# Input projection of tiles 2 to 15 in pairs by Strassen's scheme, weight sums streamed; feed-forward's second pass in two groups

## Chip, core and metric

One core of one Trainium2 chip. The metric is device microseconds (us) of one launch, the median of three runs. Everything is float32. In the trace each program matmul stands as two records.

## What is computed

One decoder layer over a prompt of 2048 tokens and 32 sample tokens (8 sequences of 4), model width 1024. The part that the change touches is the combined input projection and, in the feed-forward, only how the columns of its second pass are grouped:

```python
hn = rmsnorm(x, norm1_g[l])
proj = hn @ w_in[l]                      # (T, 1024) @ (1024, 3608)
q_a, k_a, v_a, gate_a, low_a, qkv_b, z_b, beta_b, dec_b = jnp.split(proj, IN_IDX, axis=-1)
...                                      # GLA heads and gated delta-rule heads, chunk by chunk
x = x + mix @ w_out[l]
hn2 = rmsnorm(x, norm2_g[l])
up, ffn_new = causal_dwconv(hn2 @ w_up[l], st_ffn[l], ffn_conv_w[l])
a_f, b_f = jnp.split(up, [D_FF], axis=-1)
x = x + (jax.nn.silu(a_f) * b_f) @ w_down[l]
```

## The kernel before

There are two stages, the mixers and the feed-forward, each with one hand-written instruction stream per engine. No scheduler is in it: the order in the code is the order on each engine, and semaphores join the engines.

**Mixers.** The prompt is cut into 16 tiles of 128 tokens (t = 0 to 15), and a last short tile holds the 32 sample tokens. `mixer(t)` computes both head groups of a tile, carries the two states to the next tile, and is a long chain that goes back and forth between TensorE (PE), VectorE (DVE), ScalarE (ACT) and GpSimd (POOL). The names that matter, in the order of one tile on PE: the projected row block `proj` is turned (L764, L783); the previous tile's gated output is turned (L919, which waits for DVE L1721); ACT copies the turned columns to `cx` (L1192); DVE runs the convolution's four taps (L1505, then L1507 three times), between them the decays (L1535 to L1591); ACT and DVE make the SiLU (L1262, L1614); PE turns q (L840) and the last decay (L846); ACT copies it to `ked` (L1279); PE makes the GLA output (L859, L861) and the delta rule's products (L892, L896); then a ladder of seven steps inverts a triangular matrix, in each step PE (L930) and DVE (L1740, L1767, L1771) in turn; then `uu`, the output (L1037, L1038), the norm on ACT and DVE, and the gate L1721.

Between these steps stand fillers, `fill(i, j)`, that run slots i to j-1 of 40. A slot is two program matmuls (four records), and holds work that the chain doesn't need yet. In `mixer(t)` even slots below 16 hold the output projection of tile t-1 (L730), and the 8 odd ones and slots 16 to 39 hold the input projection of tile t+1 (L696): 32 slots, 64 program matmuls of 128x451, eight weight column groups of 8 matmuls each. The whole of `w_in` (14.8 MB) stays in SBUF, in `arena`. Groups go to two PSUM banks in turn, and ACT empties each of them once, with the norm's scale, straight into `proj` (L1153).

Tile 0 is projected ahead of everything while the weights arrive. Mixers 0 to 14 each host the projection of the next tile, mixer 15 hosts that of the 32 sample tokens (L714). SyncE (SP) issues all DMAs from one queue: the output weights are loaded again for each tile in 16 chunks of 256 KB into four buffers `wo`.

**Feed-forward.** The up-projection and the down-projection already go by Strassen's scheme, in two passes over 22 column tiles of the weights. The first pass has two groups of 256 columns, the second three groups of 176; each group has the same matmuls over its own columns (L2135), and a column tile takes 28 program matmuls of it in each group. The down-projection (L2209, 128x512) is the same in both.

## Time and profile before

| | us |
|---|---|
| median of 3 runs | 3298.98 (3298.91 to 3301.03) |
| the profiled execution, time | 3301.26 |
| the profiled execution, span of the trace | 3299.5 |
| PE busy | 3198.2 (97%) |
| DVE busy | 2063.4 (63%) |
| ACT busy | 859.1 (26%) |
| POOL busy | 581.5 (18%) |
| mean granted TensorE clock | 0.982 |

The span is one execution from its first to its last instruction. Up to about 1640 us it is the mixers, then the feed-forward. Busy shares are over the whole span. What an edit inside a tile is worth is read from the timelines of one tile. Times of a tile below are those of tile 7's mixer, which PE begins at 717.89 us with L919 of the tile before.

### The profile page before, as it was taken

What the parts mean: (1) busy time and instruction counts of PE and PEld (TensorE: products, weight loads), DVE (VectorE), ACT (ScalarE), POOL (GpSimd) and SP (SyncE); (2) the same over time, 40 slices, a digit from 0 to 9 for tenths busy, and PEclk for the clock granted to TensorE, in tenths of its full rate; (3) what the DMA queues carried; (4) which work ended last, traced back from release to release, by engine and by line L of the source; (5) the groups of instructions that cost most, each with busy time, mean ns of one, the idle gap of its engine ahead of it and who ended that gap; (6) DMA issues with size and microseconds to landing.
All of it is one profiled execution on the core that took longest, in us unless ns stands there. A gap on an engine that the chain in (4) does not pass through costs nothing.

```text
span 3299.5 us, 59597 instructions
## 1 busy us (share of the span) xinstructions
PE 3198.2 (97%) x23585; PEld 2178.1 (66%) x23585; DVE 2063.4 (63%) x4876; ACT 859.1 (26%) x1897; POOL 581.5 (18%) x945
## 2 busy tenths in 40 slices
PE   7999999999999999996799999999999999999999
PEld 3555555556555555554477777777768877888775
DVE  1566665655566665655566566666686666666668
ACT  1223333233223332232322111111232222222223
POOL 1111111111111111112231121111063112111110
PEclk9999999999999999997799999999999999999999
DMA  6022222222222212215531111111133111111112
GB/s 239 9 84 84 84 65 84 84 63 67 65 79 84 84 65 84 79 53 154 156 98 39 49 53 39 39 51 39 39 114 126 39 50 40 52 39 39 40 38 77
DMA packets 225314, 236.56 MB, mean 72 GB/s; under 512 B 14268, under 2 KB 169444, under 8 KB 225043
## 3 DMA queue, kind: packets, MB, share of 16 engines
q1 hardware_dynamic: 225043, 232.81, 22.4%
q8 instruction: 187, 3.06, 0.4%
q14 instruction: 84, 0.69, 0.1%
HBM read 203.10 MB, written 29.67 MB: 71 GB/s over the span
## 4 chain that ended last, share of the span: by engine, by line
PE 48%; DVE 1%; POOL 1%; ACT 0%; issue 0%; DVEq 0%; POOLq 0%
PE mlp_bank L2135 32%; PE mlp_bank L2209 15%; PE mlp_bank L2223 2%; DVE mcv L2577 0%; POOL acc L2457 0%; PE mlp_bank L2215 0%; POOL acc L2462 0%; DVE acc L2638 0%; ACT mcv L2298 0%; PE mlp_bank L2234 0%; PE mlp_bank L2221 0%; DVE raw L2521 0%; ACT mth L2312 0%; DVE mcv L2581 0%; ACT raw L2353 0%
## 5 line engine op out<-in xcount | busy, mean ns | idle before, releaser
L696 PE MATMUL mixer_bank<-arena,hnt 128*128 128x451 f32 x2048 | 868.0, 555 | 15.5 <-DMA arena<-in_w_in_dram 8.4
L2135 PE MATMUL mlp_bank<-arena,ws 128*128 128x176 f32 (+1 forms) x3520 | 657.6, 340 | 10.6 <-ACT raw L2325 9.0
L2135 PEld LDWEIGHTS mlp_bank<-arena,ws 128*128 128x128 f32 x3520 | 588.8, 190 | 49.0 <-ACT raw L2325 10.2
L696 PEld LDWEIGHTS mixer_bank<-arena,hnt 128*128 128x128 f32 x2048 | 367.4, 191 | 307.6 <-issue 302.6
L2209 PE MATMUL mlp_bank<-arena 128*128 128x512 f32 x1120 | 493.7, 592 | 0.0
L2610 DVE TENSOR_TENSOR acc<-acc,mlp_bank 128x512 f32<-128x512 f32 x560 | 370.5, 686 | 57.0 <-PE mlp_bank L2209 54.5
L2209 PEld LDWEIGHTS mlp_bank<-arena 128*128 128x128 f32 x1120 | 211.2, 190 | 231.7 <-issue 205.3
L2577 DVE SCALAR_TENSOR_TENSOR mcv<-raw,cf,mcv 128x512 f32<-128x512 f32 (+2 forms) x440 | 287.3, 670 | 68.5 <-ACT mcv L2298 58.2
L646 POOL TENSOR_TENSOR ex<-dtt,level 128x512 f32<-128x512 f32 (+1 forms) x114 | 142.9, 1253 | 939.8 <-DVE dtt L1645 641.6
L2135 PE MATMUL mlp_bank<-arena 128*128 128x176 f32 (+1 forms) x1320 | 254.9, 343 | 5.2 <-PEq L2720 4.3
L730 PE MATMUL mixer_bank<-wo,th 128*128 128x512 f32 x512 | 249.0, 609 | 3.0 <-DMA wo<-in_w_out_dram 2.4
L2135 PEld LDWEIGHTS mlp_bank<-arena 128*128 128x128 f32 x1320 | 224.1, 192 | 41.2 <-issue 26.3
L2135 PE MATMUL mlp_bank<-arena,wu 128*128 128x176 f32 (+1 forms) x1320 | 250.3, 339 | 0.9 <-ACT raw L2327 0.9
L2135 PEld LDWEIGHTS mlp_bank<-arena,wu 128*128 128x128 f32 x1320 | 221.8, 190 | 33.2 <-issue 19.1
L1153 ACT ACTIVATE proj<-mixer_bank,x_rs 128x451 f32<-128x451 f32 x128 | 81.2, 635 | 557.7 <-PE mixer_bank L696 525.8
L2521 DVE TENSOR_TENSOR raw<-raw,mlp_bank 128x176 f32<-128x176 f32 (+1 forms) x110 | 40.9, 372 | 275.2 <-PE mlp_bank L2135 275.2
L2298 ACT ACTIVATE mcv<-raw,cf 128x512 f32<-128x512 f32 (+2 forms) x220 | 139.8, 637 | 100.7 <-DVE raw L2521 80.0
L2281 ACT COPY raw<-mlp_bank 128x176 f32<-128x176 f32 (+1 forms) x110 | 36.5, 332 | 493.2 <-PE mlp_bank L2135 493.2
L730 PEld LDWEIGHTS mixer_bank<-wo,th 128*128 128x128 f32 x512 | 93.3, 191 | 100.6 <-issue 89.2
L1507 DVE SCALAR_TENSOR_TENSOR cv<-cx,cw,cv 128x128 f32<-128x128 f32 x576 | 154.9, 348 | 0.0
L2515 DVE TENSOR_TENSOR raw<-raw,mlp_bank 128x176 f32<-128x176 f32 (+1 forms) x110 | 40.8, 371 | 151.2 <-ACT raw L2327 151.2
L1767 DVE TENSOR_TENSOR qe<-qe,mixer_bank 128x256 f32<-128x256 f32 x80 | 33.9, 423 | 126.9 <-PE mixer_bank L930 126.9
(368 smaller groups left out, 3619.3 us busy)
## 6 DMA issues: line engine op xcount, KB each, us to landing
wo<-in_w_out_dram SPq DMA_DIRECT2D x260, 256.0 KB, 2.7
arena<-in_w_up_dram SPq DMA_DIRECT2D x44, 512.0 KB, 4.9
wu<-in_w_up_dram SPq DMA_DIRECT2D x44, 512.0 KB, 4.9
arena<-in_w_down_dram SPq DMA_DIRECT2D x40, 512.0 KB, 4.1
arena<-in_w_in_dram SPq DMA_DIRECT2D x7, 1804.0 KB, 16.2
xc<-in_x_t_dram SPq DMA_DIRECT2D x16, 512.0 KB, 4.2
xt<-in_x_prompt_dram SPq DMA_DIRECT2D x16, 512.0 KB, 4.9
xr<-in_x_prompt_dram SPq DMA_DIRECT2D x16, 512.0 KB, 3.8
```

Source lines behind the costliest of these rows:

```text
L646: gp.tensor_tensor(ltm[0:N, :, 0:N], lt[0:N, :, 0:N], level[0:N, l, 0:N].unsqueeze(1).to_broadcast([N, H, N]), ALU.mult)\
L696: x = pe.matmul(bank[ring(g)][0:N, 0:GW], hnt[:, k, 0:N], w[:, k, g * GW:(g + 1) * GW], start=(k == 0), stop=(k == KT - 1))
L730: pe.matmul(bank[e if t == TILES else 0][0:N, :], mixt[k // H][:, k % H, 0:N], wo[i % 4][:, :], start=(k == 0), stop=(k == KT - 1)).then_i ...
L1153: act.activation(proj[0:N, g * GW:(g + 1) * GW], bank[ring(g)][0:N, 0:GW], ACT.Identity, scale=x_rs[0:N, :]).then_inc(s_proj_out, 1)
L1507: x = dve.scalar_tensor_tensor(out=dst, in0=src, scalar=cw[:, c, tap:tap + 1], in1=dst, op0=ALU.mult, op1=ALU.add)
L2135: x = pe.matmul(out[:, 0:N], left[:, k, :], xb[:, slot, k, g * N:(g + 1) * N], start=first and k == 0, stop=k == HK - 1, skip_group_check= ...
L2209: pe.matmul(bank[4 + o % 4][:, :], left, right, start=True, stop=True).then_inc(s_down_done, 1)
L2223: x = pe.matmul(out[0:N, :], act_[a + j][:, t * C:t * C + N], right[j][:, e * 512:e * 512 + 512], start=(j == 0 and t < 8), stop=(j == 1))
L2298: act.activation(cv[e][:, 0:n], raw[p][e][:, c0:c0 + n], ACT.Identity, scale=cf[p][:, e, 0:1])\
L2521: dve.tensor_tensor(v, v, q_bank[:, 0:N], ALU.add).then_inc(s_q2_added, 1)
L2577: x = dve.scalar_tensor_tensor(out=dst, in0=src, scalar=w, in1=dst, op0=ALU.mult, op1=ALU.add)
L2610: dve.tensor_tensor(v, v, bank[4 + o % 4][:, :], ALU.add).then_inc(s_y_added, 1)
```

## The change

**The projection.** Tiles 2 to 15 are projected in pairs (2,3), (4,5), ... as a 2 x 2 block product: rows are the two tiles, the inner dimension and the columns are halved. Seven products of 4 program matmuls of 128x451 take the place of eight, for each of four column group pairs. Mixer 2p hosts two of them and mixer 2p+1 the other two: 14 products, 56 program matmuls and 28 slots a mixer, for 64 and 32 before. Mixers 0 to 13 host (`HOSTS = 14`). Tiles 0 and 1 are projected the plain way ahead of mixer 0 (`project_first`, 128 program matmuls), mixers 14 and 15 host only the sample tokens.

**Weights.** Only the lower half of the columns stays in SBUF. The four combinations T1 to T4 of each column group are made once by DVE (16 subtractions of 128x1804) and stored to DRAM, and each mixer streams ten chunks of 924 KB (T1 to T4 and B22, for two groups) through a ring of four buffers.

**Activations.** POOL makes the seven left operands of a pair in eight instructions of 128x512 (`x_operands`), which now also takes the norm's scale, read back from DRAM. In the queue of POOL they stand between mixers 2p-1 and 2p. DVE scales the two tiles' columns by the norm's gain together, at the end of an even mixer.

**Results.** Of each 7 products ACT copies 4 blocks to a staging buffer (`keep`), and DVE adds 3 (`add_product`). Finished blocks are stored to DRAM and `proj` is loaded from there a tile later; of the odd mixers' results the first row's blocks are written to `proj` at once.

**Slots.** Slots 0, 1, 2, 3, 4, 6, 8 and 10 hold the output projection, 28 others the products; slots 13, 19, 23 and 39 are empty.

**Feed-forward.** The second pass goes in two groups of 264 columns.

The diff, cut to its core:

```diff
+HOSTS = TILES - 2
+PRODUCTS = 14
+CHUNKS = 10
+OUT_SLOTS = {0: 0, 1: 1, 2: 2, 3: 3, 4: 4, 6: 5, 8: 6, 10: 7}
+PRODUCT_SLOTS = {slot: p for p, slot in enumerate([5, 7, 9, 11, 12, 14, 15, 16, 17, 18, 20, 21, 22, 24] + list(range(25, 39)))}
...
+            def x_operands(p):
+
+                c, done = 2 * p + 2, 7 * p
+                a11, a12, a22, s1, s2, s3, s4 = (xops[:, b, :, :] for b in range(7))
+                scale = [rsb[:, e, :].unsqueeze(1).to_broadcast([C, HK_IN, C]) for e in range(2)]
+                gp.wait_ge(s_rsb_loaded, 16 * (p + 1))
+                gp.wait_ge(s_xg_made, p + 1)
+                if p:
+                    gp.wait_ge(s_products, PRODUCTS * 2 * p)
...
+                gp.tensor_tensor(a11, xc[:, 0:HK_IN, :], scale[0], ALU.mult).then_inc(s_xops_made, 1)
...
             for t in range(1, TILES):
                 mixer(t, t + 1, False, True)
+                if t % 2 and t < HOSTS - 1:
+                    x_operands((t + 1) // 2)
...
+                for k in range(2 * half, 2 * half + 2):
+                    x = pe.matmul(out[:, 0:GW], xops[:, left, k, :], right[:, k, :], start=first and k == 0,
+                                  stop=k == HK_IN - 1, skip_group_check=not first)
...
+            def keep(t, q, block, source):
+
+                act.wait_ge(s_products, PRODUCTS * t + q + 1)
...
+                act.copy(stage[4 * (q // 7) + block], bank[source][:, 0:GW]).then_inc(s_kept, 1)
...
-                fill(1)
+                if not sample:
+                    act.wait_ge(s_halo_kept, n + 1)
                 if out and not sample:
-                    act.wait_ge(s_halo_kept, n + 1)
                     y_square(t, C)
+                    act.wait_ge(s_y_normed, 3 * t - 2)
+                front(0)
...
                     if a == 1 and out and not sample:
-                        if not last_prompt:
-                            keep_y_half(t, C, 0)
+                        keep_y_half(t, C, 0)
...
+                    if half == 0:
+                        pe.wait_ge(s_sg_new, t + 1)
+                    else:
+                        pe.wait_ge(s_hs_half, t)
+                    y_turn(t, C, half)
...
                 conv_tap(2)
+                if hosts:
+                    make_c11(t, 0)
...
-        PASSES = ((0, 2, 256, 0, 8), (T // 2, 3, 176, 8, 9))
+        PASSES = ((0, 2, 256, 0, 8), (T // 2, 2, 264, 8, 9))
```

**Where it stands on the engines.** First PE, from the product with `qka` (L827 before, L1099 now) to the first GLA product (L859 before, L1135 now). L696 before and L970 now are the slots' matmuls, two to a slot; L840 and L1114 turn q, L846 and L1120 the last decay. Before:

```order
L827 MATMUL mixer_bank<-qka 32x32 x16
L696 MATMUL mixer_bank<-arena,hnt 128x451 x4
L840 MATMUL mixer_bank<-ident,cv 128x128 x4
L696 MATMUL mixer_bank<-arena,hnt 128x451 x4
L846 MATMUL mixer_bank<-ident,ex 128x128 x2
L850 MATMUL mixer_bank<-ident,cv 128x128 x4
L696 MATMUL mixer_bank<-arena,hnt 128x451 x2
L859 MATMUL mixer_bank<-va,at 128x128
```

and now:

```order
L1099 MATMUL mixer_bank<-qka 32x32 x16
L970 MATMUL mixer_bank<-arena 128x451 x4
L1114 MATMUL mixer_bank<-ident,cv 128x128 x4
L970 MATMUL mixer_bank<-arena 128x451 x2
L1120 MATMUL mixer_bank<-ident,ex 128x128 x2
L1126 MATMUL mixer_bank<-ident,cv 128x128 x4
L970 MATMUL mixer_bank<-arena 128x451 x2
L1135 MATMUL mixer_bank<-va,at 128x128
```

Slot 19 is gone between L1114 and L1120; slot 13 is gone a little earlier.

Second ACT, from the table load after the decay's exponential to the copy of `ked` (L1279 before, L1578 now), which the GLA product waits for. L1153 empties a projection bank, L1158 and L1448 square the layer's output, L1420 squares the input tokens of a later tile (before: L1139, in the ladder). Before:

```order
L1266 ACT_TABLE_LOAD
L1153 ACTIVATE proj<-mixer_bank,x_rs 128x451 [waits x_rsed,proj_done,va_copied]
L1158 ACTIVATE cx,y_ss<-yo 128x8x128 [waits out_out,halo_kept]
L1273 ACTIVATE th<-mixer_bank 128x512 [waits q_turned]
L1163 ACTIVATE y_ln<-y_ss,eps 128x1 [waits y_squared]
L1279 COPY ked<-mixer_bank 128x256 [waits sg_done,kl_turned]
```

and now:

```order
L1563 ACT_TABLE_LOAD
L1448 ACTIVATE cx,y_ss<-yo 128x8x128 [waits out_out,halo_kept]
L1420 ACTIVATE cx,x_ss<-xt 128x8x128 [waits x_loaded,y_normed]
L1572 ACTIVATE th<-mixer_bank 128x512 [waits q_turned]
L1453 ACTIVATE y_ln<-y_ss,eps 128x1 [waits y_normed]
L1578 COPY ked<-mixer_bank 128x256 [waits sg_done,kl_turned]
```

The emptying of a bank has left this place, and the square of the input tokens has come ahead of `ked`.

Third POOL, from the last ladder step of an odd mixer to the next mixer's first two instructions (L629 and L636 before, L825 and L832 now). Before there was nothing between them. Now:

```order
L842 TENSOR_TENSOR ex<-dtt,level 128x512 [waits p_done,lt_made] x2
L849 MEMSET qe 128x4x64 [waits dx_done]
L861 TENSOR_TENSOR arena<-xc,xt 128x512 [waits products,xg_made,rsb_loaded]
L862 TENSOR_TENSOR hnt<-hnt,xt 128x512
L863 TENSOR_TENSOR arena<-xc,xt 128x512
L864 TENSOR_TENSOR arena<-hnt,xt 128x512
L866 TENSOR_TENSOR arena<-hnt,arena 128x512 [waits xops_made]
L868 TENSOR_TENSOR arena<-arena 128x512 [waits xops_made]
L869 TENSOR_TENSOR arena<-arena,hnt 128x512
L871 TENSOR_TENSOR arena<-arena 128x512 [waits xops_made]
L825 COPY va<-proj 128x512 [waits sg_done,og_done,proj_loaded,blocks_added]
L832 TENSOR_TENSOR ug<-incl,gg 128x512 [waits grow_done,g_made,masks_made]
```

Eight instructions wait for the odd mixer's last product (`products`) and stand ahead of the even mixer's `ug`.

## Rows read from the trace of the kernel before

**Rows 1.** Windows: span, its length, busy us per engine, granted clock, DMA share, GB/s.

```profile
0.00:80.00 80.00, 62.16 (x172) 31.64 (x173) 11.52 (x38) 16.30 (x37) 12.71 (x46) 0.92 0.72 246
710.00:800.00 90.00, 89.31 (x954) 52.73 (x953) 57.63 (x174) 26.15 (x55) 12.94 (x15) 1.00 0.24 77
1520.00:1530.00 10.00, 5.89 (x232) 5.08 (x232) 5.29 (x16) 0.96 (x2) 3.13 (x5) 0.50 0.59 172
```

**Rows 2.** Timeline of PE, one tile: start, length, instruction, idle before and releaser.

```profile
717.89 0.66 PE L919 MATMUL mixer_bank<-ident,th 128*128 128x128 f32 x4 [0.39 <-DVE th L1721]
...
753.79 0.60 PE L840 MATMUL mixer_bank<-ident,cv 128*128 128x128 f32 x4
...
759.42 0.38 PE L859 MATMUL mixer_bank<-va,at 128*128 128x128 f32 x2
...
771.97 0.45 PE L930 MATMUL mixer_bank<-ex,qe 128*32 128x16 f32 x32
```

**Rows 3.** Timeline of DVE, the same tile.

```profile
718.88 0.57 DVE L1472 TENSOR_TENSOR drel<-proj,dtb 128x4 f32<-128x4 f32 x1
...
720.87 2.44 DVE L1505 TENSOR_SCALAR cv<-cx,cw 128x128 f32<-128x128 f32 x12 [1.21 <-ACT cx L1192]
...
724.13 0.90 DVE L1535 TENSOR_TENSOR qe<-qe 128x256 f32<-128x256 f32 x1
...
750.83 1.90 DVE L1614 SCALAR_TENSOR_TENSOR cv<-th,cv 128x512 f32<-128x512 f32 x3 [0.86 <-ACT th L1262]
...
767.95 1.20 DVE L1749 TENSOR_TENSOR qe<-ident,qe 128x512 f32<-128x512 f32 x1
...
771.51 0.41 DVE L1740 TENSOR_TENSOR ex<-mixer_bank,nbeta 128x256 f32<-128x256 f32 x1
```

**Rows 4.** Timeline of ACT, the same tile.

```profile
755.74 0.64 ACT L1153 ACTIVATE proj<-mixer_bank,x_rs 128x451 f32<-128x451 f32 x1
756.27 1.05 ACT L1158 ACTIVATE cx<-yo 128x1024 f32<-128x1024 f32 x1
...
757.98 0.37 ACT L1279 COPY ked<-mixer_bank 128x256 f32<-128x256 f32 x1
...
772.41 1.06 ACT L1139 ACTIVATE cx<-xt 128x1024 f32<-128x1024 f32 x1
```

**Rows 5.** Timeline of POOL, the same tile.

```profile
717.95 1.48 POOL L629 COPY va<-proj 128x512 f32<-128x512 f32 x1 [18.17 <-ACT proj L1153]
723.71 1.04 POOL L636 TENSOR_TENSOR ug<-incl,gg 128x512 f32<-128x512 f32 x1 [4.28 <-DVE gg L1525]
...
767.32 1.27 POOL L646 TENSOR_TENSOR ex<-dtt,level 128x512 f32<-128x512 f32 x1 [2.28 <-PE mixer_bank L946]
```

**Rows 6.** Timelines of PE and ACT, the last prompt tile.

```profile
1458.95 0.66 PE L919 MATMUL mixer_bank<-ident,th 128*128 128x128 f32 x4 [0.39 <-DVE th L1721]
...
1501.48 0.77 PE L859 MATMUL mixer_bank<-va,at 128*128 128x128 f32 x2 [4.04 <-ACT ked L1279]
...
1521.04 1.97 PE L755 MATMUL mixer_bank<-ident,xr 128*128 128x128 f32 x8 [4.72 <-ACT proj L1411]
...
1555.93 1.11 PE L919 MATMUL mixer_bank<-ident,th 128*128 128x128 f32 x4 [3.35 <-DVE th L1721]
...
1496.39 2.59 ACT L1411 ACTIVATE proj<-mixer_bank,x_rs 32x451 f32<-32x451 f32 x4
```

**Rows 7.** PE at the start, and line L787: duration, first and last start.

```profile
8.43 8.63 PE L696 MATMUL mixer_bank<-arena,hnt 128*128 128x451 f32 x16 [8.43 <-DMA arena<-in_w_in_dram]
...
34.21 36.60 PE L696 MATMUL mixer_bank<-arena,hnt 128*128 128x451 f32 x96
...
L787 PE MATMUL mixer_bank<-lowt,wa x68: 270/270/396, 73.3 to 1558.9; 16*128 16x128 f32 x64, 16*128 16x32 f32 x4
```

**Rows 8.** Chain of waits in the feed-forward: start, length, group.

```profile
1758.54 20.72 PE mlp_bank L2135 x96
...
2540.19 22.68 PE mlp_bank L2135 x152
```

More of the change, by code:

```diff
@@ L43 @@
 GROUPS = 8
+FIRST = [(g, tile) for g in (4, 0, 5, 1, 6, 7) for tile in range(2)] + [(2, 1), (3, 1), (2, 0), (3, 0)]
 PARTS = 4 * GROUPS
 GW = NIN // GROUPS
+HW = NIN // 2
+HK_IN = KT // 2
+HOSTS = TILES - 2
+PRODUCTS = 14
+CHUNKS = 10
+KEPT = 8
+ADDED = 6
+KEEP_OF = {0: 1, 2: 2, 3: 3, 6: 4, 7: 5, 9: 6, 10: 7, 13: 8}
+ADD_OF = {1: 1, 4: 2, 5: 3, 8: 4, 11: 5, 12: 6}
+FIRST_GROUPS = 2 * GROUPS
+P_T1, P_T2, P_T3, P_T4, P_B22 = range(5)
+A11, A12, A22, S1_X, S2_X, S3_X, S4_X = range(7)
+C11, C12, C21, C22 = range(4)
+OUT_SLOTS = {0: 0, 1: 1, 2: 2, 3: 3, 4: 4, 6: 5, 8: 6, 10: 7}
+PRODUCT_SLOTS = {slot: p for p, slot in enumerate([5, 7, 9, 11, 12, 14, 15, 16, 17, 18, 20, 21, 22, 24] + list(range(25, 39)))}
 O_QA, O_VA, O_GA, O_LOW, O_QKV, O_Z, O_BETA, O_DEC = 0, 512, 1024, 1536, 1552, 3088, 3600, 3604
@@ new lines, in store_block @@
+            def store_block(t, j, block):
+                b = 4 * j + block
+                if block == C11:
+                    sp.wait_ge(s_added, ADDED * t + ADD_OF[(1, 8)[j]])
+                elif block == C12:
+                    sp.wait_ge(s_added, ADDED * t + ADD_OF[(5, 11)[j]])
+                elif block == C22:
+                    sp.wait_ge(s_added, ADDED * t + ADD_OF[(4, 12)[j]])
+                else:
+                    sp.wait_ge(s_kept, KEPT * t + KEEP_OF[(6, 13)[j]])
+                c0 = HW * (block in (C12, C22)) + column_group(t, j) * GW
+                tile = t - t % 2 + 2 + (block in (C21, C22))
+                sp.dma_start(p_d[tile, :, c0:c0 + GW], stage[b]).then_inc(s_stage_stored, 16)
@@ L847, in mixer @@
                 x.then_inc(s_kl_turned, 1)
+                if not sample:
+                    pe.wait_ge(s_out_out, 2 * t)
                 for h in range(H):
@@ L1326, in mixer @@
                     norm_k()
-                    fill(3)
-                    front(0)
+                    if hosts:
+                        keep(t, 6, C21, 1)
+                    front(1)
                     inverse_rms(0, front)
-                for g in range(4, GROUPS - 1):
-                    fill(g)
+                if hosts:
+                    keep(t, 7, C11, 0)
+                    keep(t, 9, C22, 0)
+                    keep(t, 10, C12, 1)
+                if t == TILES - 1:
+                    keep_sample()
                 if sample:
```

815 lines of the change are left out of this document (540 added, 275 removed).

## The prediction

> **What bounds the kernel now.** I read the windows first. In a middle stretch of the mixers PE is busy 89.31 of 90 us at full clock, DVE 57.6, ACT 26, POOL 13 [rows 1]. That looks like a kernel bound by PE, in which each slot removed is won. The timelines of one tile say more. Its period is (1458.95 - 717.89) / 8 = 92.63 us [rows 2, 6]. A slot is four records of 36.6/96 = 0.38 us, 1.52 us [rows 7]. The question at each removed slot is how late the chain behind it would be if PE came 1.52 us earlier. So I looked, at each of the four places, for when DVE or ACT had finished what PE then used, and beside it at the last prompt tile, whose slots are almost empty, and which shows the chain bare [rows 6]. The reader should see that PE arrives only about 1 us after its data, and at two places after them.
>
> **The tile, place by place.** The change takes 4 of 32 slots from a tile, 6.06 us of PE.
>
> Slot 13 lies ahead of L840. DVE starts the taps at 720.87, after waiting for ACT, and then has work without a real break until L1614 ends at 750.83 + 1.90 = 752.73; PE comes at 753.79 [rows 2, 3]. The slack is 1.06. The change also puts the first C11 addition between the taps: a 128x451 operation is a little under the 0.7 of 128x512, 0.6. So the data are there at 753.3, and L840 moves by 0.5, not 1.5.
>
> Slot 19 lies ahead of L859, which needs `ked`. It is done at 757.98 + 0.37 = 758.35, and PE comes at 759.42 [rows 2, 4]. On ACT one emptying leaves this path (L1153, 0.53 by the starts), and the squares of the input tokens enter it (L1139's 1.06, and a short wait for the instruction ahead), which before ran at 772, where nobody waited [rows 4]. With the 0.6 from DVE: 758.35 + 0.6 - 0.5 + 1.1 = 759.5. L859 stays where it was, and both slots are lost. The last tile bears this out: there, with hardly any filler, PE waited 4.04 us for `ked`, 2.59 of it for ACT's sample blocks, and L859 came 1501.48 - 1458.95 = 42.5 us after L919, against 41.5 in the full tile [rows 2, 6].
>
> Slot 23 lies in the ladder's second step. L1740 ends on DVE at 771.92, and PE goes on at 771.97 [rows 2, 3]: DVE is the bound there already, and the slot gives nothing. Behind it `turn_y(1)` now waits for DVE's `hs_half`, which follows L1740, the new C12 addition (0.6) and a 128x512 operation: PE goes on at about 773.1 where it did at 772.65, +0.4. From there to the end of the ladder the same 13 slots stand in both kernels.
>
> Slot 39 lies ahead of L919, which waits for DVE as it is (0.39) [rows 2]. The wait becomes 1.9.
>
> So a hosted tile takes 92.63 + 0.1 + 0.4 = about 93.0 us (0.1 is from `ked`): nothing is won inside a tile. The other additions on DVE and copies on ACT lie in gaps of the ladder; C22 ahead of product 13 is one product behind its data, and the turn of `uu` (0.9 us) stands between. They cost nothing while DVE is idle there.
>
> **POOL's eight instructions.** In six of the tiles (2, 4, ... 12) they start when the odd mixer's last product ends, about 2.5 us ahead of L919, and run 8 x 1.27 = 10.2 us [rows 5]. In this time DVE runs the gate, the decay's start and the taps, on the chain. What the rows show of the two engines: L1472, four elements wide, starts at 718.88 and ends at 719.45, when POOL's copy ends (717.95 + 1.48 = 719.43); L1749 ends 0.56 after POOL's L646 at 768.59; L1535 ends at 725.03, 0.28 after POOL's L636 at 724.75 [rows 3, 5]. Each waited to the end of the POOL instruction. The bounds are 1 us a tile (POOL slips between) and 7 us (all eight block DVE, 10.2 less the 3 us in which DVE waits for ACT before the taps, now that the 1.2 us scaling has left the odd mixer's end). I take 5: about five of the eight fall on a working DVE at 1 us each. 6 x 5 = +30 us. `ug` comes later as well, at about 729 for 727.6; PE has 1.7 us to spare up to L840 and DVE is later still, so it adds nothing.
>
> The Trainium skill, "SBUF — State Buffer", section "Who interferes with whom", says that DVE's second port pair is shared with GpSimd and held exclusively for a whole instruction, by DVE operations with two SBUF inputs and also by `tensor_scalar` in a two-port mode. All three rows have two SBUF inputs; no row here shows the second kind. By it the twelve `tensor_scalar` taps of L1505 would be blocked too, and a tile would cost about 6 in place of 5; without it, about 3.5.
>
> **The ends of the mixers.** Now tile 0 alone is projected first, and L787 of tile 0 comes at 73.3 [rows 7]. After the change 256 records stand ahead of it: 8.4 start, 256 x 0.38 = 97.1, 2.5 for the low clock of the first 16 records (8.63 for 6.1), some 3 for the second tile's columns and the second group, 2.7 for the turns: 114, so +41. The loads (14.8 MB at 246 GB/s, 60 us [rows 1]) are covered. DVE's 16 subtractions, 1.9 us each by the same rate, wait for projections and stores and end by about 111, just in time; bounds of this part +36 to +46.
>
> Against it stand the last mixers. Before: 15 tiles from 73.3 to the last L787 of a prompt tile at 1460.97, and 97.9 to 1558.9 [rows 7]. Now mixers 14 and 15 have no filler. Their length is read from tile 15: 1555.93 - 1458.95 = 97.0, less the 4.7 us wait for sample blocks (L755 now goes to another bank) and the 2.6 of L1411 ahead of `ked`: 90 each [rows 6]. It is at a granted clock down to 0.50 in its second half [rows 1], to which PE fell after its idle stretches; if the clock stayed up, 80. Sum: 114 + 91.7 (mixer 0, which has no output projection and takes that now) + 13 x 93.0 + 2 x 90 = 1594.7, against 1558.9: +36.
>
> **Feed-forward.** A record takes 20.72/96 = 215.8 ns at 256 columns and 22.68/152 = 149.2 to 149.8 at 176 [rows 8]. At 264 it is 215.8 + 8 x 0.83 = 222.5. A column tile has 168 records of 176, 25.1 to 25.2 us, and then 112 of 264, 24.9: 0.2 x 22 = 5 us less (bounds +3 to -8 for the turn between the passes and the longer last group). -5.
>
> **Sum.** 36 + 30 - 5 = +61 on the profiled execution's 3301.3, that is 3362; the median is 2.3 below that execution, so 3360.
>
> **The rivals.**
> 1. *PE is the bound after all.* The busy share of 89.31 in 90 speaks for it, the waits at L840, L859, L930 and L919 against it. If every slot is won, a tile takes 86.6 and mixer 0 85.6, and POOL is hidden: 114 + 85.6 + 13 x 86.6 + 180 = 1505, -54, and -5: 3240. This is the faster side; it decides from 2.6 us a tile, at which the start-up's +36 is paid. 0.09.
> 2. *POOL slips into DVE's gaps.* Three tenths of the first 10 us are DVE waiting. 6 x 1 in place of 6 x 5: 3336. 0.25.
> 3. *The stream disturbs the chain.* DMA carries 77 GB/s, 7.1 MB a tile [rows 1]; the change adds ten chunks of 0.92 MB and 2.8 MB of blocks, to 19 MB or 206 GB/s. Rows show 246 at a share of 0.72, so it fits on average. But the 16 output weight chunks of 256 KB, with four buffers, are now used in a row in slots 0 to 4, behind a 924 KB chunk in the one queue (3.8 us at 246). If that makes PE more than the 1.7 us late that L840 forgives, say by 3 more a tile: 13 x 3 = +39, 3399. 0.14.
> 4. *Half of it.* The chain is tight at L840 and L919, but the token squares fit, and two slots are won: 13 x 3 = -39 and POOL at 3: about 3305, on either side of no change. 0.08.
>
> The forecast has 0.44. The range 3300 to 3400 holds it, rivals 2 and 3 and half of 4. A measurement tells 0.2% (6.6 us) from no change: slower has 0.44 + 0.25 + 0.14 = 0.83, same 0.04 and faster 0.13 (rival 1 and half of 4).
>
> **What would show it.** L787 of tile 0 at about 114. In a hosted tile PE waits: about 1 us at L1114 for DVE, 2 at L1135 for ACT's `ked`, 1 in the ladder's second step, 2 at L1196 for the gate; PE at 93% rather than 99%. An even tile longer than an odd one by about 5 us, with DVE operations that end when POOL's do. If odd and even tiles are alike, POOL's term is wrong; if an odd tile is under 90 us, the chain's is. Waits on `wo` at L1002 show rival 3.

## The result, and the profile after

The changed kernel takes 3429.4 us (median; 3424.3 to 3434.0), against 3298.9 for the kernel before on the same chip: a ratio of 1.0393, 95% interval 1.0380 to 1.0405. It is slower, as forecast, but the loss is 130 us where 61 were expected, and 3429 lies above the range of 3300 to 3400. The profiled execution's span is 3425.8.

The page of the changed kernel, its first parts. Columns: busy us and share of each engine; then the granted clock in 40 slices.

```profile
span 3425.8 us, 56382 instructions
...
PE 3186.7 (93%) x22129; PEld 2094.5 (61%) x22129; DVE 2132.8 (62%) x4778; ACT 825.7 (24%) x1743; POOL 640.9 (19%) x985
...
PEclk9899999999999999988689999999999999999999
```

PE is busy for 93% of the span, as the forecast said. The clock's digit is 9 through the hosted mixers, and 9 stands for 90% or more: too coarse for a few per cent. Windows are finer. These are the changed kernel's: the hosted mixers 1 to 13, mixer 0, one odd and one even tile. (Where only PE was asked for, the columns are start and end, length, PE busy, granted clock, DMA share, GB/s; else all engines stand between, as in [rows 1].)

```profile
222.90:1505.60 1282.70, 1185.29 (x12339) 0.96 0.58 188
...
111.00:222.90 111.90, 79.47 (x911) 48.16 (x910) 66.66 (x181) 23.66 (x51) 19.04 (x19) 0.83 0.64 212
809.60:908.40 98.80, 90.65 (x950) 54.24 (x949) 61.04 (x179) 26.14 (x55) 15.73 (x18) 0.96 0.55 177
908.40:1010.70 102.30, 92.61 (x951) 54.85 (x950) 66.02 (x181) 26.91 (x57) 18.77 (x21) 0.94 0.62 201
```

And the same stretch of hosted mixers in the kernel before:

```profile
164.60:1369.00 1204.40, 1195.45 (x12548) 1.00 0.24 75
```

Before, PE ran through the mixers at a granted clock of 1.00. After, it gets 0.96 on average. In 13 tiles PE has 209 records fewer, its busy time falls by only 10 us, and the stretch is 78 us longer. The sum of the forecast held PE at full clock throughout the hosted tiles.

The waits of PE in the hosted mixers 1 to 13 of the changed kernel (instruction, what it waited for: us in total, times, longest):

```profile
PE mixer_bank L1135 <- ACT ked L1578: 26.4, 13, 2.1
PE mixer_bank L1196 <- DVE th L2068: 24.7, 13, 1.9
PE mixer_bank L1065 <- DVE gg L1866: 12.5, 6, 3.8
PE mixer_bank L1027 <- DVE hgla L2042: 10.5, 13, 0.8
PE mixer_bank L1207 <- DVE ex L2087: 10.1, 13, 0.8
```

The same list of the kernel before has 5.1 us ahead of L919 (13 times 0.4) and 2.1 ahead of L930, and nothing else. All waits of the changed kernel's list add up to 96 us. Four of the five shown were forecast: about 2.1 us for `ked` in twelve of the 13 tiles (1.1 in the last) and 1.9 for the gate in each, under 1 at the two ladder steps. The fifth, for `gg`, stands in even tiles alone and is told below. The first record of each mixer (L1059, L787 before) gives the tile lengths, of one execution of each kernel:

| stretch, us | before | forecast | after | fillers (e3) | bound (e12) |
|---|---|---|---|---|---|
| start, to the first L1059 | 73.3 | 114 | 111.0 | 111.0 | 111.3 |
| mixer 0 | 90.8 | 91.7 | 111.9 | 112.1 | 103.6 |
| odd hosted tiles, mean of 7 | 92.6 | 93.0 | 97.0 | 93.7 | 94.1 |
| even hosted tiles, mean of 6 | 92.6 | 98.0 | 100.6 | 99.0 | 93.8 |
| mixers 1 to 13 together | 1204.2 | 1239 | 1282.7 | 1250.2 | 1221.5 |
| mixer 14 | 92.6 | 90 | 95.9 | 97.8 | 80.5 |
| mixer 15 | 97.3 | 90 | 90.4 | 86.5 | 89.8 |
| from there to the end | 1741.2 | 1736.2 | 1733.9 | 1737.4 | 1737.8 |
| span | 3299.5 | 3360.9 | 3425.8 | 3395.0 | 3344.6 |

(e3 and e12 are told below.) Of the 65 us by which the span missed the forecast, 43.7 lie in the hosted mixers, 20.2 in mixer 0, 6 in mixers 14 and 15; the start and the feed-forward give 5 back.

**What a clock loss looks like in rows.** PE's timeline in mixer 7 of the changed kernel, from the wait for `ked`; it answers to the row of L859 in [rows 2]:

```profile
849.94 0.46 PE L1135 MATMUL mixer_bank<-va,at 128*128 128x128 f32 x2 [2.12 <-ACT ked L1578]
...
851.35 0.63 PE L1135 MATMUL mixer_bank<-va,at 128*128 128x128 f32 x2
...
853.06 1.88 PE L1168 MATMUL mixer_bank<-cv 128*128 128x128 f32 x8
854.76 1.06 PE L1172 MATMUL mixer_bank<-cv 128*128 128x128 f32 x8
...
866.24 4.27 PE L970 MATMUL mixer_bank<-arena 128*128 128x451 f32 x8
...
893.94 3.25 PE L970 MATMUL mixer_bank<-arena 128*128 128x451 f32 x8
```

PE waits 2.12 us and runs on for 1.4 us. Then eight records of the delta rule's products take 1.88 us (L1168), and the next eight, of the same shape, 1.06 (L1172). Eight records of the projection take 4.27 us at 866 and 3.25 at 894. No wait stands inside these rows: the records themselves are longer. Windows show why (start and end, length, PE busy, granted clock, DMA share, GB/s):

```profile
851.40:854.70 3.30, 3.30 (x18) 0.50 0.00 0
854.80:858.20 3.40, 3.40 (x23) 1.00 0.00 0
```

For these microseconds the granted clock is the lower of its two levels, 1.2 in place of 2.4 GHz. This cost stands in no list of waits. It has to be read from the clock column, or from one shape that has two durations.

Read in this way, the clock of mixers 1 to 13 of the changed kernel falls 26 times, for 3 to 7 us each time: ten times at the wait for the gate, five behind the wait for `ked`, eight in the ladder's first steps, three at the wait for `gg` where that is 2.5 us or more. Together it is at the lower level for 115 of the 1282.7 us.

**Even tiles.** DVE's timeline of the even mixer 8, and POOL's beside it; they answer to [rows 3] and [rows 5]:

```profile
907.00 1.20 DVE L1816 TENSOR_SCALAR dabs<-drel 128x4 int32<-128x4 int32 x1
909.39 6.86 DVE L1846 TENSOR_SCALAR cv<-cx,cw 128x128 f32<-128x128 f32 x12 [1.19 <-ACT cx L1482]
```

```profile
904.13 1.58 POOL L861 TENSOR_TENSOR arena<-xc,xt 128x512 f32<-128x512 f32 x1 [16.00 <-PE mixer_bank L970]
...
913.51 1.32 POOL L871 TENSOR_TENSOR arena<-arena 128x512 f32<-128x512 f32 x1
```

The twelve `tensor_scalar` taps take 6.86 us where [rows 3] have 2.44, while the second half of POOL's eight instructions runs, to 914.83. So it is in each even tile that has them, 6.0 to 6.9, and in no other (2.44). PE then waits 3.8 us for `gg` (L1065), and 0.8 to 3.8 in the six tiles. The Trainium skill, "SBUF — State Buffer", section "Who interferes with whom", names `tensor_scalar` in a two-port mode as one that GpSimd can block. No row of the kernel before showed that; this one agrees, with 4.4 us on twelve instructions.

**Mixer 0.** SP's, DVE's and ACT's timelines of the changed kernel, 60 to 140 us (SPq is the queue in which SP issues DMAs). DVE waited for the stores of the weight sums, and the last sum ended at 118.71 + 4.11 = 122.8, where the forecast had 111:

```profile
63.77 19.10 SPq L509 DMA_DIRECT2D sums_d<-arena  x6
...
94.24 28.92 SPq L509 DMA_DIRECT2D sums_d<-arena  x10
123.20 0.46 SPq L622 DMA_DIRECT2D proj_d<-ex  x1
```

```profile
78.41 4.11 DVE L1730 TENSOR_TENSOR arena<-arena 128x1804 f32<-128x1804 f32 x2 [26.57 <-DMA sums_d<-arena]
...
118.71 4.11 DVE L1730 TENSOR_TENSOR arena<-arena 128x1804 f32<-128x1804 f32 x2 [3.60 <-DMA sums_d<-arena]
134.05 0.16 DVE L1860 SCALAR_TENSOR_TENSOR drel<-drel,dln 128x4 f32<-128x4 f32 x1 [8.58 <-ACT dln L1499]
```

```profile
132.76 0.63 ACT L1490 ACTIVATE qe<-mixer_bank,ba 128x128 f32<-128x128 f32 x2 [20.89 <-DMA proj_d<-qe]
```

Then DVE waited 8.58 us for ACT, ACT for the store of tile 1's projection out of `ex` and `qe`, and this store stood in SP's queue behind the last ten stores of the sums. PE waited 22.7 us at L1065.

### The profile page after: what moved, and what is told of

It is laid out like the page before. It is cut to its first block and busy times, and to the rows that moved or that the text cites. A ratio compares the mean times of both kernels' runs of the same rounds, so it can differ in the third digit from the quotient of the medians.

```text
span 3425.8 us, 56382 instructions
## 1 busy us (share of the span) xinstructions
PE 3186.7 (93%) x22129; PEld 2094.5 (61%) x22129; DVE 2132.8 (62%) x4778; ACT 825.7 (24%) x1743; POOL 640.9 (19%) x985
## 5 line engine op out<-in xcount | busy, mean ns | idle before, releaser
L970 PE MATMUL mixer_bank<-arena 128*128 128x451 f32 x1568 | 677.3, 562 | 0.4 <-issue 0.4
L2496 PE MATMUL mlp_bank<-arena,ws 128*128 128x256 f32 (+1 forms) x2816 | 648.3, 383 | 9.6 <-ACT raw L2686 9.6
L2496 PEld LDWEIGHTS mlp_bank<-arena,ws 128*128 128x128 f32 x2816 | 536.0, 190 | 92.8 <-ACT raw L2686 10.4
L970 PEld LDWEIGHTS mixer_bank<-arena 128*128 128x128 f32 x1568 | 281.6, 194 | 210.4 <-issue 204.3
L2938 DVE SCALAR_TENSOR_TENSOR mcv<-raw,cf,mcv 128x512 f32<-128x512 f32 (+2 forms) x352 | 264.5, 767 | 59.4 <-ACT mcv L2659 50.6
L1002 PE MATMUL mixer_bank<-wo,th 128*128 128x512 f32 x512 | 266.3, 651 | 18.0 <-DMA wo<-in_w_out_dram 17.1
L2496 PE MATMUL mlp_bank<-arena 128*128 128x256 f32 (+1 forms) x1056 | 249.1, 386 | 5.3 <-PEq L3084 4.4
L2496 PE MATMUL mlp_bank<-arena,wu 128*128 128x256 f32 (+1 forms) x1056 | 246.0, 383 | 0.9 <-ACT raw L2688 0.9
L2496 PEld LDWEIGHTS mlp_bank<-arena 128*128 128x128 f32 x1056 | 201.1, 191 | 57.0 <-issue 26.4
L2882 DVE TENSOR_TENSOR raw<-raw,mlp_bank 128x256 f32<-128x256 f32 (+1 forms) x88 | 37.5, 426 | 276.7 <-PE mlp_bank L2496 276.7
L1444 ACT COPY arena<-mixer_bank 128x451 f32<-128x451 f32 x112 | 59.7, 533 | 592.4 <-PE mixer_bank L970 592.3
L1002 PEld LDWEIGHTS mixer_bank<-wo,th 128*128 128x128 f32 x512 | 100.6, 208 | 142.8 <-issue 96.5
L2876 DVE TENSOR_TENSOR raw<-raw,mlp_bank 128x256 f32<-128x256 f32 (+1 forms) x88 | 37.5, 426 | 191.3 <-ACT raw L2688 191.3
L2642 ACT COPY raw<-mlp_bank 128x256 f32<-128x256 f32 (+1 forms) x88 | 33.1, 377 | 493.2 <-PE mlp_bank L2496 493.2
```

Of the source, the lines that this page charges most:

```text
L970: x = pe.matmul(out[:, 0:GW], xops[:, left, k, :], right[:, k, :], start=first and k == 0, stop=k == HK_IN - 1, skip_group_check=not first)
L1002: pe.matmul(bank[e if t == TILES else 3 + e][0:N, :], mixt[k // H][:, k % H, 0:N], wo[i % 4][:, :], start=(k == 0), stop=(k == KT - 1)).th ...
L1444: act.copy(stage[4 * (q // 7) + block], bank[source][:, 0:GW]).then_inc(s_kept, 1)
L2496: x = pe.matmul(out[:, 0:N], left[:, k, :], xb[:, slot, k, g * N:(g + 1) * N], start=first and k == 0, stop=k == HK - 1, skip_group_check= ...
L2876: dve.tensor_tensor(v, v, q_bank[:, 0:N], ALU.add).then_inc(s_q1_added, 1)
L2938: x = dve.scalar_tensor_tensor(out=dst, in0=src, scalar=w, in1=dst, op0=ALU.mult, op1=ALU.add)
```

## The experiments

Twelve kernels ran, each beside runs of the kernel before. The changed kernel's 3429.4 is the reference for those made from it.

### e1: POOL's eight operations made small

```diff
-                a11, a12, a22, s1, s2, s3, s4 = (xops[:, b, :, :] for b in range(7))
+                a11, a12, a22, s1, s2, s3, s4 = (xops[:, b, 0:1, 0:4] for b in range(7))
...
-                gp.tensor_tensor(a11, xc[:, 0:HK_IN, :], scale[0], ALU.mult).then_inc(s_xops_made, 1)
+                gp.tensor_tensor(a11, xc[:, 0:1, 0:4], scale[0], ALU.mult).then_inc(s_xops_made, 1)
...
```

> POOL's eight instructions of x_operands are made four columns wide in place of 128x512; the left operands of the products are otherwise left unmade, so the projections of tiles 2 to 15 are not the reference's. All waits and their order stay. Theory A (an even tile is longer because DVE's taps wait for these instructions, and PE then for DVE): L1846 back from 6.9 to 2.4 us in even tiles, the wait for gg at L1065 gone, even tiles as long as odd ones; 6 x 3.5 = 21 us at least, with the lower clock behind the wait some 30: 3395 to 3410 for 3429. Rival (the even tiles are longer through their DMAs, the 1.8 MB reload of proj among them): no change, 3425 to 3433.

3417.0 us (ratio 1.0346, 1.0329 to 1.0363): 12 us less, not 21 or more, so it lies between the two expectations. DVE's taps came back to 0.28 us each (0.29 at the most), 2.44 for the twelve in every tile, and the wait for `gg` is gone, so the mechanism is right. Even tiles became 2.9 us shorter and odd ones did not: they take 97.7 and 97.8 now (odd ones 97.0 in the changed kernel), at a granted clock of 0.96, the changed kernel's. The price at a full clock is measured by e11.

### e2: the token squares back at their old place

```diff
                 if out and not sample:
                     y_square(t, C)
-                    act.wait_ge(s_y_normed, 3 * t - 2)
-                front(0)
...
                     if hosts:
                         keep(t, 6, C21, 1)
+                    front(0)
                     front(1)
```

> The square of the input tokens goes back on ACT from ahead of ked to where it stood before, behind the last copy ahead of the ladder. Theory A: ked is 1.1 us earlier, the wait at L1135 falls from 2.1 to 1.0 us, 14 tiles: -15 us, and a shorter wait lowers the clock less: 3400 to 3415. Rival (the wait at L1135 is late by something other than ACT's row of work, the turn of q for instance): the wait stays at 2.1 and the time at 3429.

3410.0 us (1.0332, 1.0315 to 1.0349), 19 less, as theory A has it. The wait for `ked` fell from 26.4 to 11.9 us in 13 tiles, 1.1 us a tile, just the length of the moved square (1.06). The hosted mixers are 19.5 us shorter; the other 5 come with a clock of 0.97 for 0.96 and aren't taken apart further.

### e3: useless matmuls in PE's waits

```diff
+            def warm(count, b=0):
+                for _ in range(count):
+                    pe.matmul(bank[b][:, GW:512], ident[:, :], lo[:, 0, 0:512 - GW], start=True, stop=True,
+                              skip_group_check=True)
...
+                if 2 <= t < HOSTS and t % 2 == 0:
+                    warm(16)
...
```

> Nothing is taken away: useless matmuls of 128x61 from the identity into unused bank columns are added on PE in hosted tiles where it waits now: 8 ahead of L1135, 3 in the second ladder step, 7 ahead of L1196, 16 ahead of L1065 in even tiles. Theory A (the excess over the forecast is the granted clock, which falls behind each wait): granted clock in hosted tiles from 0.95 to 0.98 or more, hosted tiles 2 to 4 us shorter, 3380 to 3405, though PE does more. Rival (the clock costs nothing, since the tile is bound by the chain; the excess is DMA): the added 0.2 us pieces are hidden or lengthen the chain, 3429 to 3440.

3402.5 us (1.0318, 1.0301 to 1.0335), as theory A has it. The kernel has 348 program matmuls (696 records) more than the changed one, none of use, and is 27 us faster. The matmuls write into banks that hold open products, so only its time is read. Its hosted mixers (start and end, length, PE busy, granted clock, DMA share, GB/s):

```profile
223.10:1473.30 1250.20, 1207.09 (x13000) 1.00 0.60 193
...
802.40:896.10 93.70, 91.22 (x986) 1.00 0.57 188
896.10:995.30 99.20, 94.57 (x1018) 1.00 0.64 206
```

The clock is 1.00 again, and now an odd tile takes 93.7 and an even one 99.0, against 93.0 and 98.0 forecast. The clock was thus worth 32.5 of the 43.7 us by which the hosted mixers missed, by one execution of each kernel; between the medians of the two kernels lie 27 us. The traffic is as high as in the changed kernel (193 against 188 GB/s), so it is not what brings the clock down. The fillers don't set the tile's length themselves: right behind them PE still waits, 0.4 us for `ked` and 0.4 for the gate.

### e4: the stream made small

```diff
...
-                sp.dma_start(x_flat[n % 4], t_d[4 * what + j]).then_inc(s_ring_loaded[n % 4], 16)
+                sp.dma_start(x_flat[n % 4][:, 0:64], t_d[j, :, 0:64]).then_inc(s_ring_loaded[n % 4], 16)
```

> The ring's chunks of 924 KB are loaded as 64 columns of it (33 KB) each, in the same places of SP's queue and with the same semaphores; most of the right operands stay stale, so the projections of tiles 2 to 15 are not the reference's. Theory A: the stream explains little: the waits on wo at L1002 go, 0.5 to 1 us a tile at most, 3410 to 3429. Rival B (rival 3 of the prediction: the stream makes the output weights late and pushes the chain): 3 us a tile and more, 3375 to 3390.

3429.8 us (1.0400, 1.0382 to 1.0417), no change, with 101 GB/s in the hosted mixers for 188. Rival 3, the stream that disturbs the chain, falls. Its sign was missing in the changed kernel too: L1002 waited on `wo` once in these 13 mixers, for 0.6 us.

```profile
220.90:1503.10 1282.20, 1190.97 (x12338) 0.95 0.33 101
```

### e5: slots 13 and 19 filled, 22 and 24 empty

```diff
-PRODUCT_SLOTS = {slot: p for p, slot in enumerate([5, 7, 9, 11, 12, 14, 15, 16, 17, 18, 20, 21, 22, 24] + list(range(25, 39)))}
+PRODUCT_SLOTS = {slot: p for p, slot in enumerate([5, 7, 9, 11, 12, 13, 14, 15, 16, 17, 18, 19, 20, 21] + list(range(25, 39)))}
```

> The changed kernel with the products of slots 14 to 24 put on 13 to 21: slots 13 and 19 are filled, 22 and 24 stand empty. Theory A (slot 19 lies ahead of the wait for ked, 2.12 us in every tile, and slots 22 and 24 where no wait ends late): the wait for ked falls from 2.12 to about 0.4, as with the fillers, a hosted tile gets 1.5 us shorter and some more by the clock, 3395 to 3412 against 3429.4. Rival B (the work taken from 22 and 24 opens waits of the same length in the ladder of a=1 to 3, one wait goes and two come): no change or worse, 3425 to 3436.

3415.3 us (1.0350, 1.0332 to 1.0367), 14 less, inside neither span of the two expectations. Both theories were half right. These are its waits in the hosted mixers:

```profile
PE mixer_bank L1207 <- DVE qe L2096: 12.2, 13, 0.9
...
PE mixer_bank L1257 <- DVE qe L2087: 6.7, 13, 0.5
```

The wait for `ked` is gone from the list; two in the ladder came, 0.8 and 0.5 us more a tile. All waits add up to 81 us, 15 less than in the changed kernel. The clock did not rise: 0.95.

### e7: tile 1's store ahead of the last sums

```diff
             store_sum(11, P_T2, 3, y_flat[3])
+            sp.wait_ge(s_one_out, GROUPS)
+            sp.dma_start(p_d[1, :, 0:5 * GW], ex_[:, 0:5 * GW]).then_inc(s_stage_stored, 16)
+            sp.dma_start(p_d[1, :, 5 * GW:NIN], qe_[:, 0:3 * GW]).then_inc(s_stage_stored, 16)
             store_sum(12, P_T3, 2, x_flat[2])
...
```

> The changed kernel with the store of tile 1's first projection ahead of the stores of sums 12 to 15 in SyncE's queue. Theory A (in mixer 0 VectorE waited 8.6 us for ScalarE, which waited for that store, and TensorE 22.7 us for VectorE): the 8.6 us go, mixer 0 takes 103 for 111.9, the time is 3419 to 3424. Rival B (VectorE then waits for the stores of the sums instead, which come later): mixer 0 stays at 110 or more, 3427 to 3433.

3423.9 us (1.0371, 1.0354 to 1.0389), at the end of theory A's range; its four runs spread from 3419 to 3432, so the median alone does not carry the verdict. The trace does: mixer 0 takes 103.7 for 111.9, and PE's wait for `gg` there is 14.2 for 22.7, 8.5 less. In this execution the hosted mixers take 4 us more than the changed kernel's and mixer 14 3, which hides it in the time.

### e9: w_out's pieces ahead of the re-loaded w_in

```diff
-            for g in range(4, GROUPS):
-                w_group(g)
             wo_chunks(t - 1, 20)
+            for g in range(4, GROUPS):
+                w_group(g)
             load_proj(t + 1)
```

> The changed kernel with w_out's pieces of mixer 14 ahead of the four re-loaded groups of w_in in SyncE's queue, nothing else. Theory A (SyncE needs 12 us to issue the 3.6 MB of w_in, and they fill the DMA engines, while TensorE waits 14.0 us for a piece of w_out): that wait goes, mixer 14 takes 81 for 95.9, the time is 3413 to 3418. Rival B (the groups then come too late for the sample's second half in mixer 15, or the load of proj does): mixer 15 grows by what mixer 14 gives back, 3425 to 3432.

3417.6 us (1.0362, 1.0341 to 1.0383), 12 less, as theory A has it. In the changed kernel PE stood 14 us in mixer 14:

```profile
1526.45 5.74 PE L1002 MATMUL mixer_bank<-wo,th 128*128 128x512 f32 x8 [14.01 <-DMA wo<-in_w_out_dram]
```

With the edit this wait is gone and mixer 14 takes 81.5 for 95.9; mixer 15 takes 93.4 for 90.4, so 11 are left.

### e8: holes in the kernel before

All work kept; one product is done a slot later, one a slot earlier.

```diff
+                    late = {19: (), 20: (19, 20), 37: (37, 38), 38: ()}
-                    for part in range(i, j):
+                    for part in [p for slot in range(i, j) for p in late.get(slot, (slot,))]:
```

> The kernel before, all its work kept, with two holes in TensorE's stream of the kind that the change makes: the product of slot 19 is done with that of slot 20, and that of slot 38 with that of slot 37, so that TensorE has nothing to do at the places where it stands ahead of gla_out (L859) and ahead of turn_mixed(1) (L919). Each hole is about one slot, 1.5 us, so 3.0 us a tile and 43 us in 14 tiles are waited whatever the clock does. Theory A (in the changed kernel the granted clock falls because TensorE stands still for one or two us at a time): the clock of the hosted tiles, 1.00 in the kernel before, falls to 0.97 to 0.99, a tile takes 97 to 98 for 92.6, and the time is 3355 to 3380. Rival B (the clock fell in the changed kernel for something else that came with it, its traffic or its other matmuls): the clock stays at 1.00, a tile takes 95.6, and the time is 3340 to 3344.

3339.1 us (1.0122, 1.0106 to 1.0137). By the time alone rival B would nearly have won, 3340 to 3344. The trace says otherwise. Only one of the two holes opened: the wait ahead of L919 became 1.9 us (0.4 before), and no wait for `ked` appears, so 1.5 us a tile are waited and not 3.0. The expectation had read the order wrongly: slot 20 lies ahead of L859 too, so the product moved there from slot 19 left no hole.

```profile
PE mixer_bank L919 <- DVE th L1722: 24.8, 13, 1.9
```

Yet nine tiles of thirteen are 2.6 to 3.9 us longer (95.2 to 96.5), one 2.3, and only three 1.5 (94.1 or 94.2). One tile of each kind, by windows (start and end, length, PE busy, granted clock, DMA share, GB/s):

```profile
260.40:356.10 95.70, 93.50 (x967) 0.98 0.24 73
353.20:356.50 3.30, 3.30 (x16) 0.50 0.32 85
737.40:831.50 94.10, 91.89 (x966) 1.00 0.24 74
735.80:739.10 3.30, 3.30 (x21) 1.00 0.30 80
```

The short windows are the microseconds behind the wait. And PE's timeline behind two of these waits:

```profile
352.76 0.81 PE L919 MATMUL mixer_bank<-ident,th 128*128 128x128 f32 x4 [1.90 <-DVE th L1722]
353.36 2.77 PE L783 MATMUL mixer_bank<-ident,proj 128*128 128x128 f32 x12
356.06 0.92 PE L787 MATMUL mixer_bank<-lowt,wa 16*128 16x128 f32 x4
...
735.36 0.66 PE L919 MATMUL mixer_bank<-ident,th 128*128 128x128 f32 x4 [1.90 <-DVE th L1722]
735.85 1.60 PE L783 MATMUL mixer_bank<-ident,proj 128*128 128x128 f32 x12
737.38 0.71 PE L787 MATMUL mixer_bank<-lowt,wa 16*128 16x128 f32 x4
```

One kernel, one wait of 1.90 us, one row of instructions: twelve transposes take 2.77 us in one tile and 1.60 in the other. From L919 to the end of L787 it is 4.2 us against 2.7. So a wait of 1.9 us in a stream that has no other can cost 1.5 us more behind it, as much as the wait itself had grown. Over mixers 1 to 13 the kernel is 34.6 us longer than the kernel before: 20 are the longer waits, 15 what comes behind them. The granted clock, 0.99 in these mixers, falls behind nine of the 13 waits. That is theory A's mechanism in the kernel before, with none of the change in it; theory A's time was for two holes. Why the clock falls behind some of these like waits and not behind others isn't shown. The Trainium skill, "TensorE: Matmul & The Clock Gate", section "A second HAM failure mode: psum-queue depth-cycling", tells of another kernel in which TensorE idled briefly between groups of matmuls so often that the clock went back and forth between its two levels. These rows agree, with one idle of 1.90 us a tile.

### e11: small POOL operations and fillers

The edits of e1 and e3 together, without the 16 matmuls ahead of L1065.

> The changed kernel with two edits: useless matmuls in TensorE's waits (8 ahead of gla_out, 3 at step a=1, 7 ahead of turn_mixed(1)), and GpSimd's seven x_operands operations 4 columns wide, so most of that work is left out and the operands are wrong. It prices the x_operands of an even tile at full clock. Theory A (they hold VectorE's tensor_scalar back and so the hosting tile by 5 us): even tiles take 93.5 as odd ones do, 98.7 with the fillers alone, so 30 us go: 3366 to 3380 against 3402.5. Rival B (the x_operands cost mainly by the clock that their waits bring down, since they were worth 12 us alone): at a full clock there is little left to gain: 3388 to 3400.

3367.9 us (1.0202, 1.0186 to 1.0218), inside theory A. The hosted mixers take 1222.5 us for 1250.2 of e3, both at a clock of 1.00, so POOL's eight operations cost (1250.2 - 1222.5)/6 = 4.6 us an even tile. Even and odd tiles are alike now, 94.2 and 93.9.

### e10: all small mends together

The edits of e2, e5, e7 and e9, and the fillers of e3 ahead of L1065 and of `turn_mixed(1)` alone.

> The changed kernel with all the small mends together: the next tile's squares back at their old place ahead of front(1), slots 13 and 19 filled and 22 and 24 empty, tile 1's store ahead of the last sums' stores in SyncE's queue, w_out's pieces of mixer 14 ahead of the four re-loaded groups of w_in, and useless matmuls ahead of the even tiles' L1065 (16) and ahead of turn_mixed(1) (7). Theory A (the change is dearer by its start, mixer 0 and GpSimd's operands even when the clock is held): 111 + 105 + 13 tiles of 92 or 97.5 (1229) + 84 + 87 + 1736 = 3352, 3335 to 3368, still slower than before. Rival B (nearly all of the loss is the clock and mends of a few us each): 3299 or less. Rival C (the mends don't add, since each gave back the same clock): 3385 to 3400.

3377.9 us (1.0240, 1.0225 to 1.0256), between A (3335 to 3368) and C (3385 to 3400). Mixer 0 takes 102.5 and mixer 14 80.4, near A's 105 and 84. The hosted mixers take 1252 where A had 1229:

```profile
216.00:1468.00 1252.00, 1204.78 (x12714) 0.97 0.60 193
```

No wait in them is longer than 0.9 us, but the clock is 0.97: the two empty slots 22 and 24 opened short waits in a row in the ladder, as in e5. PE in the ladder of mixer 1, and a window from its last wait on:

```profile
264.50 0.66 PE L1265 MATMUL mixer_bank<-ident,qe 128*128 128x128 f32 x4 [0.52 <-DVE qe L2096]
266.09 0.45 PE L1215 MATMUL mixer_bank<-qe,ex 128*32 128x16 f32 x32 [0.94 <-DVE qe L2105]
267.34 0.69 PE L1027 MATMUL mixer_bank<-ident,xr 128*128 128x128 f32 x4 [0.81 <-DVE hgla L2051]
268.78 0.63 PE L1215 MATMUL mixer_bank<-ex,qe 128*32 128x16 f32 x32 [0.75 <-DVE ex L2096]
```

```profile
268.00:274.60 6.60, 5.78 (x106) 0.50 0.39 98
```

The waits listed for these mixers add up to 46 us; e3's, with a clock of 1.00, to 42. So the sum of the waits does not tell the clock. How close they stand tells more. Four waits of 0.3 to 0.9 us within some 5 us, as here, and the clock falls in the ladder of all 13 mixers; so it does in e5, which has the same four. Two of 0.8 us, followed in most tiles by one of 0.4 (the changed kernel), and it falls in eight of 13. One of 0.8 and one of 0.4 (e3), and it falls in none.

### e12: a bound from below

The edits of e11, e7 and e9.

> The changed kernel with four edits, for a bound from below: useless matmuls in TensorE's waits, the x_operands 4 columns wide (most of that work left out), tile 1's store ahead, w_out's pieces ahead. Against the run with the first two alone, 3367.9, the two queue edits are worth 9 and 15. Theory A (the scheme costs its start, 38 us, and mixer 0, about 10, and a hosted tile is set by VectorE's chain at 93.7 for 92.6, so that the 6 us of matmuls a tile that it saves are lost): 3340 to 3348, slower than before even so. Rival B (the last stalls hide a gain): under 3320.

3348.7 us (1.0149, 1.0131 to 1.0167), at the edge of theory A. Even with the operands' work left out, the clock at 1.00 and both queue faults mended, the scheme is 1.5% slower than before: by the table, 38 us in the start, 13 in mixer 0, 17 in the hosted mixers, against 12 in mixer 14, 7 in mixer 15 and 3 in the feed-forward. A hosted tile takes 94.0 with 6.06 us of products less in it, and PE still waits, right behind the fillers too: 0.4 us for `ked`, 0.8 and 0.4 in the ladder, 0.4 for the gate.

```profile
214.90:308.60 93.70, 91.06 (x986) 55.58 (x985) 59.88 (x182) 26.24 (x56) 13.79 (x23) 1.00 0.60 189
```

### e6: the feed-forward part alone

The kernel before, with the second pass in two groups of 264 columns. The lines left out size that stage's tiles and share out its work for two groups.

```diff
...
-        PASSES = ((0, 2, 256, 0, 8), (T // 2, 3, 176, 8, 9))
+        PASSES = ((0, 2, 256, 0, 8), (T // 2, 2, 264, 8, 9))
...
```

> The kernel before with only the feed-forward part of the change: second pass in two groups, 264 columns and with them the tiles of that stage, the projection as it was. Theory A (that part is worth its 5 to 7 us by itself, as the traces of the two kernels have it, 1741.2 against 1733.9): 3291 to 3295, ratio 0.9975 to 0.9985. Rival B (the stage was shorter in the changed kernel only because the mixer ahead of it left it other things, a colder clock or an earlier load): 3298 to 3300, no change.

3294.1 us against 3299.9 (11 and 15 runs): ratio 0.9983, 0.9974 to 0.9992, as theory A has it. It is the one version that is faster than the kernel before, if by little. The span behind the last mixer is 3293.5 - 1558.9 = 1734.6, 6.6 less than before; the mixers are as they were, 92.6 a tile.

## Why the prediction was wrong

The sign held, and so did the waits inside the tile; the sum did not, since it left out what these waits do to the clock, and made mixer 0 too short. Step by step:

**The four removed slots: right.** All four were to be lost to waits. PE waits where the prediction put them (2.12 us at L1135, 1.90 at L1196, 0.81 and 0.78 in the ladder), and at a clock of 1.00 an odd tile takes 93.7 (e3), for 93.0. That DVE and ACT set the tile is borne out by e12: with products removed and fillers in the holes it is still 1.3 us longer than before, and PE still waits for them. The token squares on the way to `ked` were worth 1.1 us in e2, as written. L1114 waited little (1.8 us in all 13 tiles, where about 1 us each was forecast).

**"So a hosted tile takes ... about 93.0 us": the step that failed.** It adds waits to a stream whose records keep their length. At a granted clock of 0.94 to 0.99, tile by tile, they don't. The forecast had read the 0.50 in [rows 1], behind idle stretches of the last tile, used it for mixers 14 and 15, and did not ask the same question at the four holes that it made in a stream at 1.00. The term is 32.5 us by e3 (1282.7 - 1250.2), 2.5 a tile, and was put at nothing; without it the time would have come out at the upper end of the range, 3397 (3402 by e3's median). e8 shows the same loss in the kernel before. The remaining 11 of the 43.7 us are 0.9 a tile and are not explained here.

**POOL's eight instructions: right.** 5 us an even tile were taken, 4.6 measured at a full clock (e11 against e3), and 3.5 as the difference of even and odd tiles in the changed kernel. The blocked `tensor_scalar` shows that the estimate by the rule of the Trainium skill (6) had its mechanism right and was too high; the one without it (3.5) was too low. Of the three rows from which the forecast read the blocking, one doesn't carry it well: L1749 ends 0.56 us after POOL's instruction and not with it.

**The start: right,** 3 us too high. 111.0 for 114.

**Mixer 0: mis-sized by 20 us.** The prediction let DVE's sums end "by about 111, just in time". Its rate was a little low (2.05 us a subtraction for 1.9), but the larger part is the stores: the first store of a sum was issued at 63.8, and DVE, whose buffers it frees, waited 26.6 us for it. The sums ended at 122.8. SP's queue issued loads until then, and up to 60 us the DMA engines were busy with them to 91 to 95%. So an earlier place in the queue alone might not have brought that store forward; no run tested it. And a second thing hung on that queue: tile 1's store behind the sums' stores, with ACT, DVE and PE waiting for it in turn. It is worth 8.2 us (e7, mixer 0 103.7 for 111.9). The other 12 are put down to the late sums by the timelines alone. The prediction had looked at loads ("covered") and not at who waits for a store that stands behind stores.

**Mixers 14 and 15: 186.3 for 180.** Mixer 15 was as forecast, 90.4. In mixer 14 two errors of opposite sign partly cancelled: it is 8.5 us shorter than forecast once nothing disturbs it (81.5 in e9), and it had a wait of 14.0 us, since the re-loading of four groups of w_in went into SP's queue ahead of w_out's pieces.

**Feed-forward: right in the number, in part by luck.** 7.3 us less in the changed kernel and 6.6 in e6, for 5. The chain of waits shows the 112 records of 264 columns of one column tile in two pieces:

```profile
2669.10 21.36 PE mlp_bank L2496 x96
...
2692.18 3.56 PE mlp_bank L2496 x16
```

21.36/96 is 222.5 ns, as forecast, and the 112 take 24.92 us. The 168 records of 176 columns took 22.68 + 2.39 = 25.07 before. That is 0.15 a column tile, so some 3 us in all, not 5. The larger gain stands at the turn between the passes, which the forecast held only as a bound: from the second pass's first matmul to its first down-projection it is 83.8 us for 88.4, in the changed kernel and in e6 alike. From there to the pass's last down-projection it is another 2.4.

**The rivals.** Rival 1 (PE is the bound, 3240) and rival 4 fall with the waits. Rival 2 falls with 4.6 us a tile where it had 1. Rival 3 came nearest in time, 3399, by the wrong mechanism: e4 with about half the traffic is no faster. Rival 4's own terms come to 3309, not 3305. The range ended at 3400 because each of its cases kept the clock. With e3's 2.5 us a tile added the forecast would have been 3392, still short by mixer 0.

**What stays open.** Which waits bring the clock down. Their sum doesn't say: e3 and e10 wait 42 and 46 us, at 1.00 and 0.97; e5 waits 15 us less than the changed kernel (81 for 96), at 0.95 for 0.96. Waits that stand close together did it more often (e10), but e8's tiles have the same single wait and two outcomes. And e1 gained 12 us where e11 has 28 for the same edit: that a slower PE lets the chain catch up would explain it, and is only argued.

## What to carry to other kernels

When a change takes filler out of a stream of matmuls that runs at full clock, price each hole twice: the wait that opens, and up to as much again behind it for the clock. Here that was 15 us beside 20 of new waits in e8, and 32 beside 89 in the changed kernel. Then look at whether several short waits come to stand close together. A saving of matmuls is worth nothing where PE already arrives within a microsecond of its data, and there the question is what else the change puts on the chain. A store that frees a buffer is a wait like any other; follow SP's queue at the program's start and at its change of stage for what stands behind what.
